# Value products of both mixers in seven products of half the width, weights moving, VectorE combining and summing

## The reference

```python
h = rmsnorm(x, norm1_g[l]) * (1.0 + sc1) + sh1
hc = rmsnorm(xc, norm1_g[l]) * (1.0 + sc1c) + sh1c
y, yc = token_mixers(h @ w_in[l], hc @ w_in[l], ...)
# w_in[l]: 1024 x (512 columns each of q, k, v, o, nq, nk, nv, and 32 gate columns)
```

## Time and profile before

| | us |
|---|---|
| median of 3 runs (lowest to highest) | 3328.34 (3328.31 to 3329.49) |
| the profiled execution's own time | 3326.89 |
| its span, first to last instruction | 3324.6 |
| PE busy (share of the span) | 3223.6 (97%) |
| PEld busy | 2447.1 (74%) |
| DVE busy | 1849.2 (56%) |
| ACT busy | 639.7 (19%) |
| POOL busy | 161.1 (5%) |
| mean granted TensorE clock | 0.992 of full speed |

### The profile page before, as it was taken

One profiled execution on the slowest core, in us unless ns is written; L12 is line 12 of the kernel. 1 busy time (PEld: TensorE's weight loads), 2 busy tenths in 40 slices (PEclk: granted clock), 3 DMA queues, 4 the chain that ended last, 5 costly groups with the idle time before them and its releaser, 6 DMA issues.

```text
span 3324.6 us, 40506 instructions
## 1 busy us (share of the span) xinstructions
PE 3223.6 (97%) x15214; PEld 2447.1 (74%) x15214; DVE 1849.2 (56%) x3731; ACT 639.7 (19%) x1371; POOL 161.1 (5%) x307
## 2 busy tenths in 40 slices
PE   7999999989999999999999999999999999999999
PEld 5888865548888888888567885444488887466887
DVE  5887832638877778877354602355288555254100
ACT  2000023421000020000341002455210001254100
POOL 0000000000000000000000100000000000000000
PEclk9999999999999999999999999999999999999999
DMA  7554422114554345543325844111144222331553
GB/s 273 164 170 156 162 70 76 39 65 154 168 165 158 108 154 175 164 158 116 100 67 199 270 151 143 57 58 50 56 160 151 83 89 76 122 95 45 162 152 103
DMA packets 115186, 422.72 MB, mean 127 GB/s; under 512 B 13040, under 2 KB 16368, under 8 KB 112976
## 3 DMA queue, kind: packets, MB, share of 16 engines
q1 hardware_dynamic: 75232, 265.32, 25.0%
q0 software_dynamic: 39504, 154.77, 14.6%
q10 hardware_dynamic: 288, 0.36, 0.0%
HBM read 418.29 MB, written 1.31 MB: 126 GB/s over the span
## 4 chain that ended last, share of the span: by engine, by line
PE 92%; DVE 3%; ACT 3%; issue 1%; DMA 1%; SPq 0%; DVEq 0%; ACTq 0%
PE PS L904 30%; PE PS L956 18%; PE PS L849 11%; PE PS L1410 6%; PE PS L1012 6%; PE PS L1390 3%; PE PS L1334 2%; PE PS L977 2%; PE PS L1252 2%; PE PS L1083 1%; PE PS L1473 1%; PE PS L1190 1%; PE PS L1484 1%; PE PS L832 1%; PE PS L762 1%
## 5 line engine op out<-in xcount | busy, mean ns | idle before, releaser
L849 PE MATMUL PS<-xn,ring 128*128 128x256 f32 (+1 forms) x1504 | 372.1, 408 | 5.2 <-ACT xn L1674 4.7
L849 PEld LDWEIGHTS PS<-xn,ring 128*128 128x128 f32 x1504 | 283.8, 190 | 90.8 <-issue 47.7
L904 PE MATMUL PS<-xn,ring 128*128 128x256 f32 x1312 | 306.9, 388 | 7.1 <-ACT xn L1665 7.1
L904 PEld LDWEIGHTS PS<-xn,ring 128*128 128x128 f32 x1312 | 251.9, 194 | 60.4 <-issue 23.2
L1410 PE MATMUL PS<-xn,arena 128*128 128x512 f32 (+1 forms) x640 | 261.9, 535 | 1.4 <-ACT arena L1897 1.4
L956 PE MATMUL PS<-xn,ring 128*128 128x256 f32 x752 | 223.7, 379 | 0.0
L2186 DVE SCALAR_TENSOR_TENSOR mix<-arena,cond,mix 128x1024 f32<-128x1024 f32 x182 | 222.6, 1278 | 0.0
L956 PE MATMUL PS<-arena,ring 128*128 128x256 f32 x784 | 202.1, 380 | 0.3
L956 PE MATMUL PS<-xn 128*128 128x256 f32 x752 | 193.0, 379 | 0.0
L1012 PE MATMUL PS<-arena,ring 128*128 (+1 forms) x864 | 186.8, 379 | 0.0
L1012 PEld LDWEIGHTS PS<-arena,ring 128*128 128x128 f32 x864 | 164.2, 190 | 22.3
(11 more groups left out here) (326 smaller groups left out, 4891.4 us busy)
## 6 DMA issues: line engine op xcount, KB each, us to landing
ring<-stream SPq DMA_DIRECT2D x500, 512.0 KB, 3.7
arena<-fed_w POOLq DMA_DIRECT2D x200, 512.0 KB, 3.9
arena<-pair_m POOLq DMA_DIRECT2D x8, 1536.0 KB, 7.2
mix<-fed_w POOLq DMA_DIRECT2D x24, 512.0 KB, 4.0
arena<-pair_n POOLq DMA_DIRECT2D x8, 1024.0 KB, 5.2
mix<-gate_sums POOLq DMA_DIRECT2D x32, 256.0 KB, 4.4
mix<-na_bias POOLq DMA_DIRECT2D x8, 512.0 KB, 4.2
h<-xT SPq DMA_DIRECT2D x1, 1024.0 KB, 6.7
```

The costliest lines, as they stand in the source:

```text
L849: m = pe.matmul(PS[:, bank, 0:tokens], ring[:, s, k * P:(k + 1) * P], xn[:, k, 0:tokens], start=k == 0, stop=k == DC - 1)
L904: m = pe.matmul(out, weights, moving, start=k == 0, stop=k == 3)
```

## The change

Each mixer's 512x1024 by 1024x512 product becomes a 2x2 by 2x2 block product with seven block products in place of eight: token blocks of 256 tokens x 512 features, weight blocks of 512 x 256. The layout puts each weight block into one unit (`unit_blocks`), so the stage still has nine units. Tokens stay stationary and weights move: per product 2 token tiles x 4 chunks of 128x128 by 128x256. VectorE makes three new weight blocks per mixer and a fourth in place (`value_prep`, 128x1024 operations), four token combinations once per stage (128x1024), and seven sums per mixer (`value_sums`, 128x512, each out of one PSUM bank into `vall`). ScalarE copies only P1. Each product has a bank of its own among 1 to 7; the second mixer's products take banks as the first mixer's sums free them. VectorE's order becomes: `value_prep(0)`, the token combinations, the gate chain, `value_prep(1)`, the sums of the first and of the second mixer. The gate columns' transposes come behind the second mixer's P2, and ScalarE's copies of them behind its P1 copy of the second mixer. The pairs' first product waits for the second mixer's first sum, its second product for all sums.

```diff
+VALUE_BANKS = ({"P1": 1, "P2": 2, "P3": 3, "P7": 4, "P5": 5, "P6": 6, "P4": 7},
+               {"P1": 1, "P2": 2, "P3": 3, "P7": 6, "P5": 4, "P6": 7, "P4": 5})
+FREE_WITH = {"P2": 1, "P3": 5, "P7": 2, "P5": 4, "P6": 6, "P4": 7}
...
# TensorE, gates
+                def product(mixer, name):
+                    u0 = ph.at.unit + 1 + 4 * mixer
+                    for u in {"P1": (0,), "P2": (1,), "P7": (2,), "P4": (3,)}.get(name, ()):
+                        unit_in(u0, u)
+                    a11, a12, s3, a22 = (ring[:, (u0 + u) % RING, :] for u in range(4))
+                    s1, s2, s4 = value_s[mixer]
+                    tokens, weights = {"P1": (xn[:, 0:4, 0:HALF], a11), "P2": (xn[:, 4:8, 0:HALF], a12),
+                                       "P3": (xn[:, 4:8, HALF:TOK], s4), "P7": (comb3, s3), "P5": (value_t1, s1),
+                                       "P6": (comb2, s2), "P4": (comb4, a22)}[name]
+                    if name == "P3":
+                        pe.wait_ge(v_prep, 2 * G + mixer + 1)
+                    if name in ("P7", "P5", "P6", "P4") and mixer == 0:
+                        pe.wait_ge(v_comb, 4 * G + ("P7", "P5", "P6", "P4").index(name) + 1)
+                    if mixer:
+                        if name == "P1":
+                            pe.wait_ge(v_copied, 2 * G + 1)
+                        else:
+                            pe.wait_ge(v_summed, 14 * G + FREE_WITH[name])
+                    for t in range(2):
+                        for k in range(4):
+                            m = pe.matmul(PS[:, VALUE_BANKS[mixer][name], t * 256:(t + 1) * 256],
+                                          tokens[:, k, t * P:(t + 1) * P], weights[:, k * 256:(k + 1) * 256],
+                                          start=k == 0, stop=k == 3)
+                            if (mixer, name, k, t) == (0, "P1", 0, 0) or (mixer, name, t) == (1, "P1", 0) or \
+                                    (mixer, name, t) == (1, "P4", 0) and k < 3:
+                                m.then_inc(weights_used, 1)
+                    m.then_inc(v_made, 1)
...
# TensorE, mlstm_products and pairs
+                    if x == DC and isinstance(p, int) and p == 0:
+                        pe.wait_ge(v_summed, 14 * ph.at.gates)
...
-                pe.wait_ge(v_copied, 8 * ph.at.gates)
+                pe.wait_ge(v_summed, 14 * ph.at.gates - 6)
...
# ScalarE, gates
+                    act.wait_ge(v_made, 14 * G + 7 * mixer + 1)
+                    bank = PS[:, VALUE_BANKS[mixer]["P1"], :].rearrange("p (t n) -> p t n", t=2)
+                    act.activation(vall[:, mixer, 0:2, 256:512], bank, ACT.Copy).then_inc(v_copied, 1)
...
# VectorE, gates
+                def value_prep(mixer):
+                    a11, a12, a21, a22 = (ring[:, weights_here(ph, 1 + 4 * mixer + u), :] for u in range(4))
+                    w1, w2, w4 = value_s[mixer]
+                    n = mark(tt(w1, a21, a22, ALU.add))
+                    tt(a21, a11, a21, ALU.subtract)
+                    marked(n)
+                    link(tt(w2, w1, a11, ALU.subtract))
+                    tt(w4, a12, w2, ALU.subtract).then_inc(v_prep, 1)
...
+                    def add(n, out, name, other):
+                        dve.wait_ge(v_made, done + PRODUCTS.index(name) + 1)
+                        if n > 2:
+                            dve.wait_ge(v_summed, done + n - 1)
+                        tt(out, p(name), other, ALU.add).then_inc(v_summed, 1)
+                    dve.wait_ge(v_copied, 2 * G + mixer + 1)
+                    add(1, c11, "P2", c21)
+                    dve.wait_ge(v_summed, done + 1)
+                    add(2, c21, "P6", c21)
+                    add(3, c12, "P5", c21)
+                    add(4, c22, "P7", c21)
+                    add(5, c12, "P3", c12)
+                    add(6, c21, "P4", c22)
+                    add(7, c22, "P5", c22)
+                    dve.wait_ge(v_summed, done + 7)
...
+                dve.wait_ge(norm_out, last.at.nout + 2 * DC)
+                value_prep(0)
+                tt(comb3, b22, b12, ALU.subtract).then_inc(v_comb, 1)
+                tt(value_t1, b12, b11, ALU.subtract).then_inc(v_comb, 1)
+                dve.wait_ge(v_comb, 4 * G + 2)
+                tt(comb2, b22, value_t1, ALU.subtract).then_inc(v_comb, 1)
+                dve.wait_ge(v_comb, 4 * G + 3)
+                tt(comb4, b21, comb2, ALU.subtract).then_inc(v_comb, 1)
...
+                value_prep(1)
+                value_sums(0)
+                value_sums(1)
```

More of the change, by code:

```diff
@@ L358, in build @@
         pair_s1, pair_s2, pair_s4 = probs, probsT, wt0
+        value_t1 = sa[:, :, :].rearrange("p a (b n) -> p (a b) n", n=HALF)
+        value_s = [[t[:, :, :].rearrange("p a n -> p (a n)") for t in (probs, probsT, wt0)],
+                   [arena[:, 2 * j:2 * j + 2, :].rearrange("p a n -> p (a n)") for j in range(3)]]
         tok_flat = tok[:, :, :].rearrange("p a n -> p (a n)")
@@ L453, in build @@
         gate_cols = sem("gate_cols")
-        v_acc = sem("v_acc")
+        v_prep = sem("v_prep")
+        v_comb = sem("v_comb")
+        v_made = sem("v_made")
         v_copied = sem("v_copied")
+        v_summed = sem("v_summed")
         pm_acc = sem("pm_acc")
@@ L1382, in gates @@
                 pe.wait_ge(ada_done, ph.at.ada)
-                for mixer in range(2):
[L1384 to L1397, removed]
+                G = ph.at.gates
@@ L1398, in gates @@
+                for mixer in range(2):
+                    for name in PRODUCTS:
+                        product(mixer, name)
+                        if (mixer, name) == (1, "P2"):
                             gate_columns(ph)
@@ L1900, in gates @@
                         act.activation(g_guard, g_guard, ACT.Exp, scale=-1.0).then_inc(gate_guard, 1)
[L1901 to L1906, removed]
+                act.wait_ge(gate_turned, G + 1)
+                turned = PS[:, 0, :].rearrange("p (t e n) -> p t e n", t=4, e=2)
+                cols = arena[:, 9, :].rearrange("p (t e n) -> p t e n", t=4, e=2)
+                act.activation(cols[:, :, 0, :], turned[:, :, 0, :], ACT.Copy, scale=-1.0).then_inc(gate_cols, 1)
+                act.activation(cols[:, :, 1, :], turned[:, :, 1, :], ACT.Copy).then_inc(gate_cols, 1)
             def pairs(ph):
@@ L2563, in gates, with value_sums @@
                 o, _ = COLS[("b_gate", ph.layer)]
+                last = PLAN[PLAN.index(ph) - 1]
+                def value_prep(mixer):
[6 more added lines that the diff above has]
+                    tt(w4, a12, w2, ALU.subtract).then_inc(v_prep, 1)
+                def value_sums(mixer):
+                    p = lambda name: PS[:, VALUE_BANKS[mixer][name], :].rearrange("p (t n) -> p t n", t=2)
+                    c11, c12, c21, c22 = (vall[:, mixer, 2 * b:2 * b + 2, 256 * a:256 * a + 256]
+                                          for a in range(2) for b in range(2))
+                    done = 14 * G + 7 * mixer
+                    def add(n, out, name, other):
[13 more added lines that the diff above has]
+                    dve.wait_ge(v_summed, done + 7)
+                b11, b12, b21, b22 = (xn[:, 4 * k:4 * k + 4, e * HALF:(e + 1) * HALF] for k in range(2) for e in range(2))
+                dve.wait_ge(norm_out, last.at.nout + 2 * DC)
[6 more added lines that the diff above has]
+                tt(comb4, b21, comb2, ALU.subtract).then_inc(v_comb, 1)
                 dve.wait_ge(gate_mm, G + 1)
@@ L2722, in unit_tm, with unit_blocks @@
     return w.reshape(DC * n // UNIT, UNIT // n, P, n).transpose(0, 2, 1, 3).reshape(-1, P, UNIT)
+def unit_blocks(w):
+    return w.reshape(2, 4, P, 2, 256).transpose(3, 0, 2, 1, 4).reshape(4, P, UNIT)
 def unit_rows(w):
```

5 lines of the change are left out of this document (1 added, 4 removed).

## The result

| | before | after |
|---|---|---|
| median, us | 3328.91 (3328.31 to 3330.03, 4 runs) | 3311.24 (3307.76 to 3313.32, 4 runs) |
| profiled execution, us | 3326.89 | 3313.32 |
| its span, us | 3324.6 | 3311.3 |

The account below looks back on a forecast made before the run. TensorE, busy for 97% of the span, was taken as the bound. Two stages saving 7.51 us each give 15.0: 3326.89 - 15.0 = 3311.9, plus 1.45 for a median, 3313.3 us; range 3311.0 to 3318.5.

Parts of the forecast that it names:

- The record step: TensorE's value products: 0.2159 us per record of 256 columns, read from the up projection, in place of 0.429.
- A stage: First value product to the pairs' first product: 49.11 us in place of 56.62, so 7.51 us saved per stage.
- The wait ahead of the pairs: TensorE's wait for ScalarE's fourth copy before the pairs' first product: 0.96 us per stage, forecast to go.
- Charged to each pass: Value products, alternative count: fixed cost on each of four passes, saving 6.34 us a stage in place of 6.55.
- the gate chain: VectorE in the first stage: starts 1.8 us late behind the new combinations, ends at 2050.2, nothing on the path.
- the late copy of the second stage: ScalarE's copy of the pairs' first product: 1.9 us late in the second stage, at no cost.
- T: End of the second mixer's P4, forecast at 2083.7 us in the first stage and 2878.7 in the second.
- A: Rival, chance 0.10: a VectorE wait of one or a few us reaches TensorE; 3315.2 us, up to 3318.5.
- B: Rival, chance 0.04: VectorE becomes the bound, its new operations at twice their price; 3330.7 us, no change seen.
- C: Rival, chance 0.03: weight loads of 0.190 us stand bare in the value products; slower, 3398 us.
- D: Rival, chance 0.03: as many columns as before in the products, only the wait gone; 3326.4 us.
- The step that failed: Pairs stage behind the gates stages: nothing takes a fixed time, so the end moves by the same 15.0 us.

Follow-up runs that it names:

- experiment 2: Kernel before with only its wait for ScalarE's value copies moved behind the pairs' first products: median 3327.74 us, ratio 0.9993.
- experiment 6: Changed kernel with two more additions into a scratch tile ahead of each of VectorE's sums: median 3323.55 us, ratio 0.9985.
- experiment 4: New form in the first gates stage only, the second stage as in the kernel before: median 3318.94 us, ratio 0.9968.
- experiments 2 and 8: experiment 2, and: changed kernel padded to the old stage length, 3328.32 us; kernel before with four or seven idle matmuls in the first stage, 3325.05 and 3335.6 us.
- experiment 5: Six matmuls with no reader added at each norm, on both kernels: 3323.23 us on the kernel before, 3307.53 us on the changed one.
- padded_after: Changed kernel with idle matmuls padding both gates stages back to the old length: 3328.32 us, ratio 0.9994.
- aimed_pad: Changed kernel with 18 idle matmuls of 256 columns and two of 64 behind the first stage's last product only: 3318.42 us, one execution.
- experiments 5 to 7: experiment 5, experiment 6, and the kernel before once more, unchanged, one execution: 3331.23 us.

## Why the prediction was right in kind and short in size

**What held.** The record step: 0.2159 forecast from the up projection, 0.2159 measured. A stage: 49.11 forecast, 49.19 and 49.18 measured. The wait ahead of the pairs: gone, and worth 0.85 alone (experiment 2) where the sum had 0.96. Both stages: 15.02 forecast, 14.87 measured; the difference is 0.08 a stage: the 16 records behind the transposes last 3.72 us and not 3.62, and the transposes take 0.02 less. The kernel before has the same 0.10 there: its first record behind the transposes lasts 0.697 in place of 0.592 us and the next one starts that much later. The forecast had counted it as part of the wait, and so as gone. Charged to each pass, the 2.5 ns that the Trainium skill gives for each matmul (TensorE: Matmul & The Clock Gate, "Wait — 56ns, not 53.3ns?") would have made the products save 6.34 a stage rather than 6.55; the trace, with a step unchanged at 0.2159, is with the charge per record.

**VectorE and ScalarE.** From the start of the stage, the gate chain started 1.5 us late (1.8 forecast) and ended at +15.3 (15.6). The second mixer's combinations ended at +20.0 (20.4). Sums, masks, weights and the late copy of the second stage came at T + 1.7, T + 1.7, T + 6.2 (6.0) and 2 us late at no cost (1.9). SP waited for the value products fewer times and longer each: 99.0 us in 6 waits over both stages, the longest 23.6, against 104.4 us in 16, the longest 7.6. PE waited for no weight in either stage.

**The rivals.** A did not occur, and its arithmetic is sound: with sums three times as long, the second product waited where and as long as it should (experiment 6). B did not occur: VectorE's 128x1024 operations took 1.21 to 1.23 us each, the price of the rows, and it has room for more, since the stages stay at 49.19 with the sums tripled (experiment 6); no run made the combinations themselves slower. C: 224 weight loads of 0.190 us stand beside records of 0.216 without a gap, so 88% of the step is no more visible than 44% was. The Trainium skill (TensorE: Matmul & The Clock Gate, "The mechanism") says in one place that a load overlaps running matmuls only when its row group differs, and in another that a load into the background weight buffer is pulled ahead as well. By this trace the first alone doesn't hold: these loads use all rows, and PE has no gap. D: the wait alone gives 1.7 us in the stages, and 0.9993 [0.9984, 1.0002] in time.

**The step that failed** is one sentence: "The pairs stage behind takes nothing at a fixed time, all its waits hang on these engines, so the end moves by the same." The waits do all hang on these engines, but the clock does not. Between the stages the same instructions took 738.32 us before and 735.46 after, in two profiles of each, and 2.86 us on top of 14.87 is 17.73, against 17.67 between the medians (so close by luck: the interval of the result's ratio is 12.3 to 24.0 us). Shown is where they lie (one stretch at half clock less behind the idle 2.7 us at 2343, a shorter one at the norm at 2408); that they come in whole with the first stage alone (experiment 4); that profiles of the old form with other arrival times lie at 734.8 to 737.0 too (experiments 2 and 8); and that with most of the half clock gone at the norms the stretch between is no longer shorter with the new form, while the difference of the medians, 15.7, fits 14.87 without excluding 17 (experiment 5). So this part of the gain does not need the new form: old products with another arrival show it too. It is the kernel before that stood badly against the clock's changes.

**What stays open.** What sets the places at which a given idle time does or doesn't lower the clock. Neither the length of the stage (padded_after) nor the distance from the last stretch at half clock (aimed_pad) brought 738.32 back. And a profile shows one execution: in experiments 2 and 8 the medians (1.7 and 1.4 us below before) show less than the sections of the profile do (4.3 and 2.7), so the stretch between may differ there from run to run; no run could show that.

**The range** was the second mistake. Its low end gave 1.45 us to the scatter of executions and 0.6 to the step. The same kernel before took from 3322.6 to 3334.1 us in the 23 runs beside experiments 5 to 7, and the first section alone differs by 4.4 us between its two profiles. A change that moves all later code should have had 3 us below the sum for the stretch between alone, which gives 3310.3 and would still have missed 3310.0 by 0.3; the 4.4 us of the first section give 3308.9, which holds it.

## What to carry to other kernels

The saving inside a stage can be read from record steps of the same shape elsewhere in the trace, to 0.1 us here, even where a wait vanishes and another engine takes on 24 us of work a stage; name the slack of each new wait, since a slack that is right can be tested by tripling the work in front of it. But here, with idle times of 1.5 to 3.3 us on TensorE, code that was not changed came out 2.9 us shorter once the code ahead of it had changed, so compare windows of the unchanged code before crediting the change, and take the range from two profiles of the same kernel. Such half-clock time can be removed by itself: six matmuls with no reader at each norm were worth 6 us before (3329.34 to 3323.23) and some 4.5 after (3312.08 to 3307.53, measured in different sets of runs).

## What the runs showed of the hardware that was not expected

- Idle times alike in length, at the same place of the program, are followed by half clock in one kernel and not in the other: 2.67 us at 2342 before (clock 0.59 over 2343.0 to 2347.2), 2.68 us at 2339 after (1.00 over 2339.0 to 2343.0).
- The half-clock stretches between the stages last between 3.4 and 10.2 us, longer than any single idle time of 1.5 to 2.7 us at which they lie. One idle time of 5.10 us inside the pairs was followed by one of 6.8 us (experiment 6).
- The filled kernels do 60 matmuls more and are faster. Between the stages PE's busy time stayed (712.76 before, 711.59 filled) with 24 records more, and the stretch fell from 738.32 to 732.36.
- Dependent VectorE sums of 128x512 that read PSUM ran four in 3.08 us and two in 1.49: 0.69 each and a step of 0.8, not the 0.72 that the prediction took from two rows. It cost nothing here.
